# Level products of the linear attention: six places with one level each, where three held two each

## The reference, cut to what matters

```python
h = rmsnorm(x, pre_mix_g[l])
proj = h @ w_in[l]
o_sb = head_rmsnorm(stick_breaking_attention(sb_q, sb_k, sb_v), sb_norm_g[l], SB_HEADS)   # 6 heads x 64
o_rw = rwkv7_time_mix(...)                                                                # 6 heads x 64
o_gla = gla_linear_attention(...)                                                         # 4 heads, dk 32, dv 64
mixed = jnp.concatenate([o_sb, o_rw, o_gla], axis=-1) @ w_out[l]
x = x + rmsnorm(mixed, post_mix_g[l])
ff = jnp.square(jax.nn.relu(rmsnorm(x, pre_ffn_g[l]) @ w_ff1[l])) @ w_ff2[l]
x = x + rmsnorm(ff, post_ffn_g[l])
```

```python
b = jnp.cumsum(la_c, axis=2)                       # log decays, cumulated over the chunk
diff = b[:, :, :, None, :] - b[:, :, None, :, :]   # frame t against frame s <= t
decay = jnp.exp(jnp.where(causal[:, :, None], diff, -jnp.inf))
scores = jnp.einsum('bhtk,bhsk,bhtsk->bhts', q_c, k_c, decay)
o_intra = jnp.einsum('bhts,bhsv->bhtv', scores, v_c)
S = S * exp(b_last) + jnp.einsum('bhsk,bhsv->bhkv', k_c * jnp.exp(b_last - b), v_c)
```

```python
log_1m_beta = jnp.where(mask, jax.nn.log_sigmoid(-z), 0.0)
between = lax.cumsum(log_1m_beta, axis=3, reverse=True) - log_1m_beta
weights = jnp.where(mask, jnp.exp(jax.nn.log_sigmoid(z) + between), 0.0)
```

## Time and profile before

| | us |
|---|---|
| median of 3 runs | 1433.52 |
| the runs | 1431.35, 1433.52, 1433.65 |
| the profiled execution | 1432.52 |
| its span, first to last instruction | 1430.8 |

### The profile page before, as it was taken

How to read it: one execution, slowest core, us unless ns; L and a number is a source line. 1 busy time by engine, 2 the same in 40 slices (tenths; PEclk the granted TensorE clock), 3 DMA queues, 4 the chain that set the end, 5 groups by cost and what they waited for, 6 DMA issues and landing times. The chain is left out here.

```text
span 1430.8 us, 27701 instructions
## 1 busy us (share of the span) xinstructions
PE 1356.4 (95%) x11020; PEld 1063.1 (74%) x11020; DVE 871.6 (61%) x1347; ACT 675.3 (47%) x1249; POOL 324.6 (23%) x434
## 2 busy tenths in 40 slices
PE   7999989999899999899999889999999999999997
PEld 5877767877677665555677678888887788888886
DVE  6344261575753465667365887776665656669866
ACT  5533241352422487878354645445443434345541
POOL 6675544542432042436101300000000000000000
PEclk9999999999999899999999999999999999999999
DMA  6555333523225330304242255444443755787952
GB/s 202 148 157 150 104 82 89 150 75 79 77 74 120 130 76 6 87 4 143 89 150 103 80 169 159 142 148 157 157 138 141 282 196 178 254 273 250 300 189 114
DMA packets 191547, 201.08 MB, mean 141 GB/s; under 512 B 36670, under 2 KB 127995, under 8 KB 191419
## 3 DMA queue, kind: packets, MB, share of 16 engines
q1 hardware_dynamic: 145132, 169.47, 37.6%
q10 hardware_dynamic: 46286, 29.84, 7.5%
HBM read 145.06 MB, written 54.20 MB: 139 GB/s over the span
## 5 line engine op out<-in xcount | busy, mean ns | idle before, releaser
L484 POOL TENSOR_TENSOR fr_wL<-fr_raw,fr_wH 128x256 fp32r<-128x256 f32 (+1 forms) x208 | 163.7, 818 | 79.7 <-PE fr_ps_F L1278 57.3
L1278 PE MATMUL fr_ps_F<-fr_hL,fr_wH 128*128 128x512 f32 (+1 forms) x416 | 169.0, 406 | 2.9 <-DVE fr_hL L805 2.4
L1278 PE MATMUL fr_ps_F<-fr_hH,fr_wH 128*128 128x512 f32 (+1 forms) x416 | 166.9, 401 | 0.0
L1278 PE MATMUL fr_ps_F<-fr_hH,fr_wL 128*128 128x512 f32 (+1 forms) x416 | 113.2, 401 | 0.0
L1278 PEld LDWEIGHTS fr_ps_F<-fr_hL,fr_wH 128*128 128x128 f32 (+1 forms) x416 | 77.0, 185 | 22.8 <-issue 3.1
L2637 PE MATMUL all_ps_b<-ro_hH,ro_slot 128*128 128x512 f32 x272 | 88.5, 391 | 3.0 <-ACT pl_p L2133 1.5
L1278 PEld LDWEIGHTS fr_ps_F<-fr_hH,fr_wL 128*128 128x128 f32 (+1 forms) x416 | 76.3, 187 | 19.7 <-issue 1.5
L1278 PEld LDWEIGHTS fr_ps_F<-fr_hH,fr_wH 128*128 128x128 f32 (+1 forms) x416 | 77.1, 185 | 17.9 <-issue 1.7
L478 POOL CAST fr_wH<-fr_raw 128x1024 fp32r<-128x1024 f32 (+1 forms) x42 | 48.0, 1143 | 161.3 <-PE fr_ps_F L1278 141.3
L2646 PE MATMUL all_ps_b<-ro_hH 128*128 128x512 f32 x312 | 75.9, 389 | 0.0
L2646 PE MATMUL all_ps_b<-ro_y 128*128 128x512 f32 x300 | 72.7, 390 | 0.5 <-DVE ro_y L2467 0.5
(11 more groups left out here) (483 smaller groups left out, 3114.2 us busy)
## 6 DMA issues: line engine op xcount, KB each, us to landing
pl_slot<-in_w_ff SPq DMA_DIRECT2D x88, 256.0 KB, 4.4
pl_slot<-second_operands SPq DMA_DIRECT2D x75, 256.0 KB, 3.6
fr_raw<-in_w_in ACTq DMA_DIRECT2D x37, 512.0 KB, 4.2
second_operands<-pl_hL SPq DMA_DIRECT2D x64, 256.0 KB, 2.0
pl_hT<-in_w_ff SPq DMA_DIRECT2D x44, 256.0 KB, 4.4
projected<-fr_stage ACTq DMA_DIRECT2D x39, 256.0 KB, 4.4
pl_hT<-second_operands SPq DMA_DIRECT2D x37, 256.0 KB, 3.8
pl_xt<-in_w_ff SPq DMA_DIRECT2D x16, 512.0 KB, 5.7
```

Source lines behind the costliest of these rows:

```text
L484: m = pool.tensor_tensor(wL[b][:, k:k + 2, 0:wd], raw[b][:, k:k + 2, 0:wd], wH[b][:, k:k + 2, 0:wd].bitcast(F32), ALU.subtract)
L1278: m = pe.matmul(F[b][0:wd, :], w[b][:, k, 0:wd], a[:, k, :], start=(at_ == 0), stop=(at_ == len(passes) - 1))
```

## The change

TensorE's list has six pieces level0 to level5 in place of three, at slots 13, 14, 16, 17, 19 and 20 in place of 13, 16 and 19. Each issues the 32 matmuls of one level. A piece waits for the keys of its own level alone. The wait for the takes stands before each even level but the first, as before. The semaphore `g_level_mm` is still raised once for a pair, now by the last matmul of the odd level. Nothing else is edited: the slots and waits on the other engines are the same.

```diff
-        SLOTS = {"gate": 0, "turn_v": 3, "diag": 6, "turn_k": 9, "kv": 11, "level0": 13, "level1": 16, "level2": 19,
+        SLOTS = {"gate": 0, "turn_v": 3, "diag": 6, "turn_k": 9, "kv": 11, "level0": 13, "level1": 14, "level2": 16,
+                 "level3": 17, "level4": 19, "level5": 20,
                  "out": 22, "sums": 25,
...
-                    for two in range(3):
-                        yield h, f"level{two}"
-                        w("g_keys", h * NL + 2 * two + 2)
-                        if two:
-                            w("g_taken", 2 * (h * NL + 2 * two))
-                        else:
+                    for n in range(NL):
+                        yield h, f"level{n}"
+                        w("g_keys", h * NL + n + 1)
+                        if n == 0:
                             w("g_kv")
-                        for lv in range(2):
-                            n = 2 * two + lv
-                            d = g.D[n % 4]
-                            for c in range(CH):
-                                for hd in range(GH):
-                                    at = lv * (HALF // 2) + c * (C // 2)
-                                    mm = 1 << n
-                                    m = pe.matmul(G[hd % 2][side(hd // 2), at:at + C // 2]
-                                                  .rearrange("p (b m) -> p b m", m=mm),
-                                                  d[group(hd), chunk(c)], second(d[group(hd), chunk(c)], mm),
-                                                  start=True, stop=True)
-                        m.then_inc(s("g_level_mm"), 1)
+                        elif n % 2 == 0:
+                            w("g_taken", 2 * (h * NL + n))
+                        d, mm = g.D[n % 4], 1 << n
+                        for c in range(CH):
+                            for hd in range(GH):
+                                at = (n % 2) * (HALF // 2) + c * (C // 2)
+                                m = pe.matmul(G[hd % 2][side(hd // 2), at:at + C // 2]
+                                              .rearrange("p (b m) -> p b m", m=mm),
+                                              d[group(hd), chunk(c)], second(d[group(hd), chunk(c)], mm),
+                                              start=True, stop=True)
+                        if n % 2:
+                            m.then_inc(s("g_level_mm"), 1)
```

## The result

Over 12 runs of each on the same chips the changed kernel takes 1440.64 us (median, 1434.65 to 1445.01) and the kernel before 1433.99 us (1430.27 to 1441.14). The ratio is 1.0045, with a 95% interval of 1.0032 to 1.0059: slower by 6.4 us. The forecast was 1438.8 us: a change of 5.8 us, added to a point between the profiled execution and the median. The profiled execution took 1437.94 us, its span 1436.2 us. TensorE is busy 1357.3 us in it (before 1356.4), VectorE 872.1 (871.6): the work is the same.

A forecast was written before the change was run, and what follows sets the result against it. TensorE was taken to set the pace in the attention stretch. Late takes add 3.8 and 2.0 us; 5.8 on the profiled 1432.52 gives 1438.3, on the median 1439.3; forecast between, 1438.8 us, own range 1435.5 to 1441.5.

The forecast's parts named there:

- The bound: Stretch of the first half's level products: TensorE, busy 27.38 of 29.00 us, sets the pace with 1.6 us of slack.
- Pair 0/1: Level products 0 and 1 in attention: take0 starts later; first half's sums of unit 20 at 534.01, not 533.61.
- Pair 2/3: Level products 2 and 3, first half: take2 late, TensorE idles 1.0 us at unit 23; delay +1.28 at unit 24.
- Pair 4/5: Level products 4 and 5, first half: take4 late, TensorE idles 1.5 us before unit 26; half ends +3.8 us.
- rival (c): Attention stage: new TensorE waits bring clock dips of 1.4 us each; two dips give 1441.6 us; chance 0.11.
- The sum: Attention stage: +3.8 us in the first half and +2.0 in the second, 5.8 together; forecast's chance 0.60.
- (a): Absorbed: attention delays do not reach the end, as ScalarE would limit anyway; +1.9 us, 1434.9; chance 0.18.
- (b): Faster: in attention, half blocks hold back ScalarE's exponentials for less time; -2.5 us, 1430.5; chance 0.11.

The follow-up runs named there:

- soft_g moved: On the changed kernel, VectorE's soft_g moved from slot 19 to 20, in front of take4; ratio to the kernel before 1.0037.
- the whole pairs stand late: On the kernel before, its three uncut pieces of two levels each moved a slot later, to 14, 17, 20; ratio 1.0103.
- the control: The kernel before, unchanged, run and profiled again; ratio 0.9998, first stretch 27.76 us, second 16.12.

## Why the prediction was right, point by point

**The bound.** Right. TensorE had 1.6 us of slack in the stretch, and pauses of 1.29, 0.96, 1.73 and 1.30 us went straight into its length. VectorE's idle time, forecast near 4 and 3 us before take2 and take4, was 4.90 and 5.31.

**Pair 0/1.** Forecast: sums of unit 20 at 534.01. Measured on the same clock: 534.15. Alone it costs 0.35 us. In the second half, forecast 612.86; measured 614.25, which is 613.00 when set back by the 1.25 us between the two first blocks there. Alone it gives a second stretch of 17.25 us, where 17.2 was expected.

**Pair 2/3.** Forecast: sums of unit 23 at 543.48; measured 543.84. Forecast: sums of unit 24 at 547.20; measured 548.40. This is the term that was mis-sized. From the start of softplus 24 to its sums I took 1.60 us, from unit 20, where only a take ran beside the copy and did not slow it:

```profile
532.86 0.60 POOL L3329 COPY sb_E<-sb_row 1x512 f32<-1x512 f32 x1 [2.49 <-DVE sb_E L3461]
```

In the changed order soft_g follows that softplus at once, because ScalarE has its logarithm long ready, and the copy runs beside it: 2.43 us (539.81 to 542.24). The row of 1.07 us in the earlier trace rows, a copy beside the key cut, was the hint, and I used it only where it stood. The same 0.9 us came back at unit 26 of the second half (624.99 to 627.41 is 2.42 us).

The Trainium skill, "SBUF — State Buffer", section SBUF: two separate sides, says that a VectorE instruction with two inputs in SBUF and a GpSimd instruction that reads SBUF share one pair of ports as an exclusive lock, so that the later one waits for the whole of the other. The rows agree: soft_g, which reads two inputs in SBUF, holds VectorE from 540.41 to 541.63, and the copy that starts at 540.63 ends 0.47 us after it and lasts 1.47 us where it takes 0.60 alone. Beside takes, which read one input from PSUM, the copy took 0.60.

**Pair 4/5.** Unit 26's wait was forecast at 1.5 us and is 1.30. Alone the pair costs 2.03 us; the forecast's sum for it alone was 1.9. The 1 to 1.5 us that I later expected of it in the second half, for that pair alone, were wrong (-0.3): take4 has no softplus of this stretch behind it there, and the stall did not recur. The prediction's own sum had no such term. It had left open whether the 0.85 us before the sums of unit 26 recur, which would have made the half +2.8; they did not, and the measured +2.8 to +2.9 came from contention at unit 26 in their place (with soft_g moved the second stretch is 18.31 us, 2.0 to 2.2 over the kernel before). That this figure was met is luck.

**The clock**, rival (c), which had 0.11, came in part: one dip in the first half, 1.5 and 1.3 us, in the two profiles of the changed kernel. It is not a rule of the pause's length that the runs show. It fell behind pauses of 0.96 and 1.73 us in the changed kernel, behind 0.97 and 0.79 where pair 2/3 alone is late, and did not behind 0.96, 0.86 and 1.30 with soft_g moved, nor behind 0.95, 3.00 and 1.30 where the whole pairs stand late. What decides in a single case stays open. The Trainium skill, "TensorE: Matmul & The Clock Gate", section HAM oscillation, tells of a kernel whose waits for data throttle the clock again and again. The dips behind new pauses agree with it in kind only: its example has longer waits than the 1.40 us ahead of the row at 605.5, with which I had said that it agrees, and the 3.00 us pause passed at full clock.

**The sum.** Forecast +3.8 and +2.0 us; measured in the profiles +6.5 and +2.8 to +2.9 (the second between the sums of units 21 and 27). The medians differ by 6.6 us, and the intervals of the two ratios reach from 4.6 to 11.8 us. So the total was met more closely than its terms, and that is in part luck: about 3.6 us of contention, clock and interplay were missing. As far as the four profiles show, what stood against them is the clock elsewhere in the stage. Counted with its first block the second half is 25.39 us in the changed kernel, 22.46 in the first profile of the kernel before and 23.75 in the control, where the clock around that block was at half for longer; so the loss there is 1.6 to 2.9 us, and that of the whole stage at an equal clock 7.0 to 7.7. Nothing of it is given back behind the stage.

**Rivals (a) and (b).** Absorbed: no, the pauses were not. Faster: what is left of it is at most 0.2 us in the first half, which six pieces in the old slots give too, and 0.5 in the second, seen only when the takes stand later and about as large as a stall that goes with the whole block. Cutting work up does bring the even level forward, but VectorE waited for the odd one. The advice of the Trainium skill that the prediction quotes for cutting work up is about instructions of ScalarE and VectorE, while the change cuts up TensorE's. A signal for each level, the other way to bring take0, take2 and take4 forward, was not tried and stays open: both levels of a pair lie in the same two banks, so VectorE would read a bank while TensorE writes it.

## What to carry to other kernels

Before work is moved later in one queue, look in each queue that waits for it at what stands *behind* the waiting instruction, and count how much the moved engine has left to do before it needs that in turn. Here the answer took 2.3 to 3.4 us and TensorE had 1.0 to 2.6 us of work, and a move of one unit cost 6.4 us; moving the waiting instruction one unit too took all of it away. Take a copy's duration not from its quiet row but from what will run beside it in the new order.

## What the runs showed of the hardware

A row copy of one partition and 512 columns on GpSimd takes 0.60 us alone, and the same beside a VectorE take, which reads one input from PSUM. It takes 1.07 us when it starts 0.10 us into a VectorE subtraction of 0.70 us with both inputs in SBUF, and 1.47 us when it starts 0.22 us into soft_g, which takes 1.22 us. It works both ways: the second subtraction, started while that copy ran, takes 1.45 us (540.96 in the kernel before) where the first takes 0.70.

The granted clock stayed at 1.2 GHz from 630 to 654 us in the kernel with whole pairs late, though TensorE's records are busy throughout from 632 on, with small matmuls of 32 columns between 634.8 and 638.5. In the same profile it was full behind a pause of 3.00 us. What decides this the runs do not show.

A stall of 0.3 to 0.8 us without a releaser stands before the last two matmuls of one block of 128 in every profile that has the whole block in that place (six of them). Its cause is open.
